# Page products between scores and transposes, K heads turned first, sigmoids in pairs

## The reference

```python
q, k, v, z, xbc, dt = _split_proj(rmsnorm(h, g_mix), w_in)
# head group A: differential attention, 8 heads, two softmax maps each, causal, ALiBi
w = softmax(q1 k1 + bias) - lam * softmax(q2 k2 + bias);  o = w @ v, RMSNorm by head
# the sample tokens do the same over cache_k[page_table], cache_v[page_table] and their new row
# head group B: depthwise convolution over 4 tokens, SiLU, then a chunked Mamba-2 scan
xbc = silu(conv_b + sum(xpad[:, j:j + t] * conv_w[j] for j in range(4)))
g = y * silu(z), grouped RMSNorm
h = h + concat(o, g) @ w_out;  then a squared-ReLU MLP, a gated input embedding, a final RMSNorm
```

## Time and profile before

| | |
|---|---|
| median of 3 runs | 2903.13 us (2899.71 to 2905.94) |
| the profiled execution's own time | 2902.28 us |
| its span in the profile | 2900.2 us |
| the touched stage | about 568 to 850 us of the span |
| PE busy over the span | 2709.5 us (93%) |

### The profile page before, as it was taken

One profiled execution on the slowest core, in us unless ns is written; L12 is line 12 of the kernel. 1 busy time (PEld: TensorE's weight loads), 2 busy tenths in 40 slices (PEclk: granted clock), 3 DMA queues, 4 the chain that ended last, 5 costly groups with the idle time before them and its releaser, 6 DMA issues.

```text
span 2900.2 us, 50080 instructions
## 1 busy us (share of the span) xinstructions
PE 2709.5 (93%) x21661; PEld 2564.9 (88%) x21661; DVE 1346.2 (46%) x1501; ACT 806.7 (28%) x988; POOL 578.0 (20%) x279
## 2 busy tenths in 40 slices
PE   7999999956675899999999999999999999999998
PEld 7999999912234899999999999999999999999998
DVE  4278878528558622443333333333334333336433
ACT  3111111228752321322222222222222222223322
POOL 0099999100006110000000000001000000001322
PEclk9999999978886899999999999999999999999999
DMA  4388888398832222233333333333332333332323
GB/s 130 117 290 273 282 297 286 115 333 276 275 113 66 104 81 81 88 104 101 102 95 95 97 100 102 96 95 104 101 102 88 102 97 101 96 95 86 97 89 116
DMA packets 294895, 396.42 MB, mean 137 GB/s; under 512 B 14773, under 2 KB 256051, under 8 KB 292982
## 3 DMA queue, kind: packets, MB, share of 16 engines
q1 hardware_dynamic: 271688, 380.23, 40.7%
q10 hardware_dynamic: 22990, 13.01, 1.5%
HBM read 377.71 MB, written 15.58 MB: 136 GB/s over the span
## 4 chain that ended last, share of the span: by engine, by line
PE 80%; DVE 7%; POOL 4%; DMA 3%; issue 3%; SPq 2%; ACT 1%; ACTq 0%; DVEq 0%; POOLq 0%
PE ps L1161 25%; PE ps L1163 25%; PE ps L1166 25%; POOL kpage L1012 3%; PE ps L1261 2%; DMA kpage<-in_cache_k 1%; DMA vpage<-in_cache_v 1%; DVE wl L1628 1%; DVE se L1785 1%; PE ps L1328 1%; PE ps L1516 1%; PE ps L1310 1%; SPq L468 1%; DVE dl L1981 0%; ACT wh L600 0%
## 5 line engine op out<-in xcount | busy, mean ns | idle before, releaser
L1161 PE MATMUL ps<-uh,wh 128*128 128x260 f32 x4512 | 1184.8, 284 | 17.3 <-DVE wl L1628 13.7
L1163 PE MATMUL ps<-ul,wh 128*128 128x260 f32 x4512 | 1180.8, 283 | 0.0
L1628 DVE TENSOR_TENSOR wl<-raw,wh 128x1024 fp32r<-128x1024 f32 (+1 forms) x418 | 575.7, 1378 | 1247.7 <-ACT wh L600 1247.1
L600 ACT ACTIVATE wh<-raw 128x1024 fp32r<-128x1024 f32 (+1 forms) x418 | 440.9, 1055 | 1801.4 <-PE ps L1166 1760.5
L1166 PE MATMUL ps<-uh,wl 128*128 128x260 f32 x4512 | 907.8, 283 | 0.0
L1161 PEld LDWEIGHTS ps<-uh,wh 128*128 128x128 f32 x4512 | 853.3, 189 | 19.9 <-DVE wl L1628 10.2
L1163 PEld LDWEIGHTS ps<-ul,wh 128*128 128x128 f32 x4512 | 851.4, 189 | 0.0
L1166 PEld LDWEIGHTS ps<-uh,wl 128*128 128x128 f32 x4512 | 696.4, 189 | 0.0
L1161 PE MATMUL ps<-hh,wh 128*128 128x260 f32 x2048 | 536.2, 283 | 0.0
L1163 PE MATMUL ps<-hl,wh 128*128 128x260 f32 x2048 | 534.1, 282 | 0.0
L1166 PE MATMUL ps<-hh,wl 128*128 128x260 f32 x2048 | 410.6, 282 | 0.0
(11 more groups left out here) (341 smaller groups left out, 1570.9 us busy)
## 6 DMA issues: line engine op xcount, KB each, us to landing
kpage<-in_cache_k SPq DMA_DIRECT2D x128, 512.0 KB, 4.8
vpage<-in_cache_v SPq DMA_DIRECT2D x128, 512.0 KB, 5.1
raw<-in_w_up SPq DMA_DIRECT2D x128, 512.0 KB, 3.7
raw<-in_w_down SPq DMA_DIRECT2D x128, 512.0 KB, 3.4
raw<-in_w_in SPq DMA_DIRECT2D x88, 512.0 KB, 4.6
raw<-in_w_out SPq DMA_DIRECT2D x32, 512.0 KB, 3.5
raw<-in_w_ple_gate SPq DMA_DIRECT2D x32, 512.0 KB, 3.4
xt<-in_x_prompt SPq DMA_DIRECT2D x8, 1024.0 KB, 8.9
```

Source lines behind the costliest of these rows:

```text
L600: A(wh[:, c % 2, 0:elems], raw[:, c % 2, 0:elems], ACT.Copy).then_inc(hi_ready, 1)
L1161: mm(ps[:, bank + 2 * m + f, 0:HALF], h_, xh[:, f * HALF:(f + 1) * HALF], start=st, stop=False)
L1163: mm(ps[:, bank + 2 * m + f, 0:HALF], h_, xl[:, f * HALF:(f + 1) * HALF], start=False, stop=False)
L1628: tt(wl[:, c % 2, 0:elems], raw[:, c % 2, 0:elems], wh[:, c % 2, 0:elems].bitcast(F32), ALU.subtract).then_inc(lo_ready, 1)
```

## The change

It does four things.

1. In the loop, PE's order in a step becomes `scores(s)`, `page_values(s + 4)`, `turn(s - 2)`.
2. In the opening all eight K heads are turned before the V heads. The page products follow the turned heads number 6, 10, 14 and 16 instead of 4, 8, 12 and 16.
3. On SP the store of K follows pages 2, pages 3 and 4 follow that store, pages 5 and 6 follow the small stores, and the reload of `z` lies between pages 6 and 7.
4. ACT makes two sigmoids in every second step (6, 8, to 24), DVE the two products with them in steps 7, 9, to 25. `yb` and `eb` have four buffers each; `yb` moves to the place of `wl`, which is free then.

```diff
-        yb = sb("yb", [3, T], F32, "UH", 32768)
-        eb = sb("eb", [2, T], F32, "UH", 39008)
+        yb = sb("yb", [4, SEQ], F32, "WL")
+        eb = sb("eb", [4, T], F32, "UH", 32768)
...
-            for u in range(2, 5):
-                value_pages(u, None)
+            value_pages(2, None)
             sp.wait_ge(s_kto, NH)
             sp.dma_start(d_out["k_prompt"][0, 0]...
+            for u in range(3, 5):
+                value_pages(u, None)
             sp.wait_ge(s_vto, NH)
...
+            for u in range(5, 7):
+                value_pages(u, None)
             sp.wait_ge(s_zout, 16 * 5)
             sp.dma_start(pj[:, TZ:TZ + 8, :], z_scr.rearrange("t p n -> p t n")).then_inc(z_in, 16)
-            for u in range(5, 8):
-                value_pages(u, None)
+            value_pages(7, None)
...
# ACT: a_tap and a_sigmoid (both: j % 4 buffers, and a wait for the product of unit j - 4)
-                if 5 <= s < JOBS + 5:
+                if s % 2 == 0 and 6 <= s < JOBS + 6:
+                    a_sigmoid(s - 6)
                     a_sigmoid(s - 5)
...
# PE, opening
-            for t in range(NH):
-                for base_t, b, got, out in ((TK, 2 * t % 4, s_kto, s_kt), (TV, (2 * t + 1) % 4, s_vto, s_vt)):
+            for t in range(2 * NH):
+                base_t, out = (TK, s_kt) if t < NH else (TV, s_vt)
...
+                    page_values(0)          # after t == 5
...
-                if t % 2:
-                    page_values(t // 2)
+                if t in (9, 13):
+                    page_values(t // 4 - 1)
+            page_values(3)
...
# PE, loop
                     scores(s)
+                if s < UN - 4:
+                    page_values(s + 4)
                 if 2 <= s < UN + 2:
                     turn(s - 2)
-                if s < UN - 4:
-                    page_values(s + 4)
...
# DVE
-                if 6 <= s < JOBS + 6:
+                if s % 2 and 7 <= s < JOBS + 7:
+                    silu(s - 7)
                     silu(s - 6)
```

More of the change, by code:

```diff
@@ L649, in _ @@
             A(kstok[0:NB, :].rearrange("p (b n) -> p b n", b=2), ps[0:NB, 4:6, :], ACT.Copy).then_inc(s_kso, 1)
-            for t in range(NH):
[L651 to L655, removed]
+            for t in range(2 * NH):
+                tok, turned, done = (ktok, s_kt, s_kto) if t < NH else (vtok, s_vt, s_vto)
+                act.wait_ge(turned, t % NH + 1)
+                A(tok[:, :, t % NH * P:(t % NH + 1) * P], ps[:, t % 4, :].rearrange("p (q n) -> p q n", q=QB),
+                  ACT.Copy).then_inc(done, 1)
+                if t == 3:
                     act.wait_ge(s_rt3, 3)
@@ L658, in _ @@
                         .then_inc(s_vso, 1)
-                if t == 2:
+                if t == 6:
                     act.wait_ge(s_rt3, 4)
@@ L696, in a_tap @@
                     act.wait_ge(s_out, 16 * 6)
-                if j >= 3:
-                    act.wait_ge(c_m, j - 2)
-                A(yb[:, j % 3, 0:SEQ], pj[:, TX + j, 0:SEQ], ACT.Identity,
+                    act.wait_ge(w_used, SL_OUT + 2)
+                if j >= 4:
+                    act.wait_ge(c_m, j - 3)
+                A(yb[:, j % 4, 0:SEQ], pj[:, TX + j, 0:SEQ], ACT.Identity,
                   bias=gcol[:, G_CB + j:G_CB + j + 1],
@@ L703, in a_sigmoid @@
             def a_sigmoid(j):
-                if j >= 2:
-                    act.wait_ge(c_m, j - 1)
+                if j >= 4:
+                    act.wait_ge(c_m, j - 3)
                 if j < CT:
@@ L711, in a_sigmoid @@
                     act.wait_ge(c_v, j + 1)
-                    A(eb[:, j % 2, 0:SEQ], yb[:, j % 3, 0:SEQ], ACT.Sigmoid).then_inc(c_e, 1)
+                    A(eb[:, j % 4, 0:SEQ], yb[:, j % 4, 0:SEQ], ACT.Sigmoid).then_inc(c_e, 1)
                 else:
@@ L715, in a_sigmoid @@
                         act.wait_ge(z_in, 16)
-                    A(eb[:, j % 2], pj[:, TZ + j - CT, :], ACT.Sigmoid).then_inc(c_e, 1)
+                    A(eb[:, j % 4], pj[:, TZ + j - CT, :], ACT.Sigmoid).then_inc(c_e, 1)
             def head_root(h, q_=hq, bank=5, n=SEQ):
@@ L1266, in _ @@
             pe.wait_ge(s_vso, 1)
-            for t in range(NH):
-                for base_t, b, got, out in ((TK, 2 * t % 4, s_kto, s_kt), (TV, (2 * t + 1) % 4, s_vto, s_vt)):
[L1269 to L1275, removed]
+            for t in range(2 * NH):
+                base_t, out = (TK, s_kt) if t < NH else (TV, s_vt)
+                if 4 <= t < NH + 4:
+                    pe.wait_ge(s_kto, t - 3)
+                elif t >= NH + 4:
+                    pe.wait_ge(s_vto, t - NH - 3)
+                for q in range(QB):
+                    last = pe.transpose(ps[:, t % 4, q * P:(q + 1) * P], pj[:, base_t + t % NH, q * P:(q + 1) * P],
+                                        ident)
+                last.then_inc(out, 1)
+                if t == 3:
+                    pe.wait_ge(s_kso, 1)
+                    for k in range(8):
+                        last = pe.transpose(ps[0:NB + 3, 4 + k // 4, k % 4 * P:(k % 4 + 1) * P],
+                                            pj[:, TX + k, SEQ - 3:T], ident)
+                    last.then_inc(s_rt3, 1)
+                if t == 5:
                     pe.wait_ge(s_wz, 1)
@@ L1282, in _ @@
                     last.then_inc(s_nv, 1)
[L1283 to L1289, removed]
+                    page_values(0)
+                if t == 6:
                     pe.wait_ge(s_vso, 2)
@@ L1820, in taps @@
                     back = 3 - k
-                    y_ = yb[:, j % 3, back:SEQ]
+                    y_ = yb[:, j % 4, back:SEQ]
                     ins = stt_(y_, pj[:, TX + j, 0:SEQ - back], cwcol[:, k * CT + j:k * CT + j + 1], y_,
@@ L1832, in silu @@
                 n = SEQ if j < CT else T
-                e_ = eb[:, j % 2, 0:n]
+                e_ = eb[:, j % 4, 0:n]
                 if j < CT:
-                    tt(pj[:, TX + j, 0:SEQ], yb[:, j % 3, 0:SEQ], e_, ALU.mult).then_inc(c_m, 1)
+                    tt(pj[:, TX + j, 0:SEQ], yb[:, j % 4, 0:SEQ], e_, ALU.mult).then_inc(c_m, 1)
                 else:
```

## The result

The changed kernel takes 2881.37 us as the median of 4 runs (2879.91 to 2882.57), the kernel before 2903.68 in the same comparison. The ratio is 0.9924 with a 95% interval of 0.9907 to 0.9942: 22 us faster, where 27 were forecast (2876), inside the range of 2863 to 2892. Its profiled execution has a span of 2880.8 us.

The account below looks back on a forecast made before the run. The prediction took a ring of PE, DVE and ACT as the bound, with the ring of page buffers next. 7.5 + 4.4 + 3.5 + 11.6 = 27.0 us off 2902.28 gave 2875.3, median 2876, range 2863 to 2892.

Parts of the forecast that it names:

- opening: Stretch before the loop: K turned first and SP's new order were to win 7.5 us, bounds 0 and 10.8.
- the ring of the engines: In the loop PE, DVE and ACT hand one unit round; PE's own ring was to shrink to 5.0 us plus 0.9.
- the ring of page buffers: In the loop, two buffers freed, loaded and used in turn; to decide the unit where DVE is light, load 9.5 us.
- units 4 to 9: Loop stretch of six units: 6.37 us each, 38.2 instead of 42.6 us, 4.4 us won.
- 10 to 15: Loop units where DVE is nearly full: to fall to DVE's 47.96 us plus some 0.7 of gaps, 3.5 us won.
- 16 to 27: Loop stretch of twelve units: 6.16 us each, 73.9 instead of 85.5 us, 11.6 us won.
- the last four: Last four steps of the loop, 28.6 us: no product there, order kept, 0 won.
- half of load + 0.14 + product: Price of a loop unit with two page buffers: 6.37 us in units 4 to 9, 6.16 in 16 to 27.
- a sign of being wrong: One of the listed signs against the forecast: a page buffer's free-to-landed time above 10.5 us.
- 10.8 us of slack: From 577.6 to 635.2 us, 19.4 MB at 415 GB/s would take 46.8 us instead of 57.6; 7.5 to be recovered.
- The clock didn't stay up: Rival: PE stays at 2.4 GHz, all products take 1.92 us, 36 to 39 us won, 2865; chance 0.14.
- The transfers gave nothing back: Rival: both buffers' loads overlap more and slow down, 0 to 5 us won, 2898 to 2903; chance 0.10.

Follow-up runs that it names:

- x_loop: The kernel before with only the page product moved ahead of the turn in the loop; 2886.95 us, ratio 0.9933 to the kernel before.
- x_half: The changed kernel loading only the first 512 of 1024 columns of each value page; 2855.78 us, ratio 0.9835 to the kernel before.
- x_pairs: The kernel before with only sigmoids and their products in pairs, four buffers; 2903.74 us, ratio 0.9997 to the kernel before.
- x_idx: The changed kernel with SP looking up a group's four page numbers before waiting for the free buffer; 2881.81 us, ratio 0.9920 to the kernel before.

## Why the prediction was right

The mechanism held: the product left the ring of the engines, the ring of page buffers took over and priced the units, and ACT's saving was worth nothing by itself. The sizes by stretch, as means of the two profiles of each kernel, are: opening 5.1 us won (7.5 forecast), units 4 to 9 3.2 (4.4), 10 to 15 2.7 (3.5), 16 to 27 11.1 (11.6), the last four, to PE's first matmul after the loop, 0.6 (0; 27.8 and 27.8 before, 26.7 and 27.8 after). That is 22.6 for 27.0.

- **Edit 1.** Right: half of load + 0.14 + product gives (9.6 + 0.14 + 2.6) / 2 = 6.2 where 16 to 27 took 6.0 to 6.3 a unit. The load of 9.5 was 9.5 to 9.7 in units 16 to 27; in groups 8 to 13 it was 10.5 and 10.7, because SP was still issuing for the other buffer when one came free (1.6 to 2.1 us late in three of the six) and because `z` was in flight when group 8 was asked for (13.3 us). The prediction had a free-to-landed time above 10.5 us as a sign of being wrong, and here it was one: with the products' 2.4 and 2.6 us in place of 3.11 the formula gives 6.6 and 6.7 us a unit for the 6.37 forecast, and 6.3 and 6.8 were measured. That is what units 4 to 9 lack. The wait of the turn for DVE was to fall under 20 us; it is 24.5 and 24.6.
- **Units 10 to 15.** The wait for scores went as forecast, and what DVE has to do is the stretch (47.9 us busy of 49.4 and 49.6). x_loop shows that edit 4 has its part in this, as the prediction had it: with single sigmoids DVE waited 1.9 us for ACT, with pairs 0.1 and nothing (1.0 in the still faster x_half). A small misreading: 69 to 71% busy, which the prediction sets beside a clock of 0.80 to 0.84, leaves out these units, in which PE was busy 57% at 0.84.
- **Edits 2 and 3.** The mis-sized term. 7.5 of 10.8 us of slack were to be recovered; it was 5.1. K's store came 12 us earlier, as forecast, but PE's waits for pages in the opening did not shrink (27.3 us for 25.9). The bytes that could fill the early part aren't there: with two buffers page group 2 can't be asked for before the first product ends, and that now ends later after group 1's issue (9.7 us after it, before 8.9), so the DMA engines idle a third of the time until 587 (busy share 0.66). The sum let the bytes run at 415 GB/s throughout; they did so only from 592 us on (410 to 419 until 632).
- **Edit 4.** Priced at 0, and 0.0 us by the medians alone (x_pairs); 2 to 3 us in company by the medians, which the intervals don't tell from none. The Trainium skill ("ScalarE: Activation LUTs", What ACT_TABLE_LOAD costs) has a drain of 1.38 us at each switch. ACT's saving was 25.8 us of busy time for twenty loads, 1.29 each. A drain could hide in idle time, but after the ten loads ahead of its sigmoids ACT idles 0.1 us in all (L715 and L719 of the changed kernel), so here too the trace shows the load and no drain.
- **The rivals.** The clock didn't stay up: 0.90, 0.85 and 0.81 in the three stretches, 0.79, 0.83 and 0.81 in the second profile, 0.80, 0.84, 0.84 before. PE's waits for pages took the place of those for DVE, and the product after one of 4.43 us took 3.64 us (744.20 in the timeline above) at a granted clock of 0.50, the next one, after no wait, 1.92 us at 1.00. By the Trainium skill's rule ("TensorE: Matmul & The Clock Gate", HAM oscillation) closing the gaps keeps the clock up; the trace doesn't speak against it, for the gaps were not closed but moved. The transfers gave nothing back in units 16 to 27, where the load's mean stayed under 10 us, and about 1 us in units 4 to 9, as said under edit 1.
- **Luck.** Every priced term came out below its forecast, so nothing large was cancelled by an opposite error. But the first profile alone has 4.9 us for units 4 to 9 (4.4 forecast) and 9.7 for 16 to 27 (11.6), so the closeness of a single stretch of one profile to its forecast proves little. The sum over units 4 to 27, 16.9 us won for 19.5, is the firmer figure.

## What to carry to other kernels

When an engine waits inside a ring of engines, independent work of the same engine belongs into that wait; but work out first the next ring, here the one of the buffers that this work consumes, for it sets what is won. Taking 18% of its work from an engine that is busy three quarters to four fifths of the time brought nothing by itself; with shorter units around it, it began to count a little. A load's issue time and the transfer of what was issued before overlap: shortening one alone may show nothing, so test both, and test a bound by halving its bytes as well as by adding to its cost, since the addition may make a new bound.

## What the runs showed of the hardware

- Four 512 KB DMAs issued in 1.6 us instead of 3.6 landed at almost the same time (9.4 us after the buffer came free for 9.5 to 9.7): the last took 7.3 us from its issue on average instead of 5.6, at 392 GB/s where both buffers' loads followed each other closely and 284 over units 16 to 27 (x_idx). With half the bytes the last landed 3.0 us after its issue.
- The last matmul of the unchanged input projection ended anywhere from 567.7 to 574.3 us over the 14 profiles; the two executions of the kernel before are the two ends of that range. A single span holds this variation in full. Why it varies was not tried.
- SP needs 1.2 us for one page's look-up and DMA, 1.75 with a second look-up, 0.5 without one between.
